# Half steps of the recurrence levels, 16-token blocks first, and two heads' matmuls in turn, in a hybrid decoder step

## The reference

```
s = einsum('btngd,btknd->btngk', q, k_sel) * 64**-0.5 ; p = softmax(s)      # attention over the chosen keys
o = einsum('btngk,btknd->btngd', p, v_sel)

b = cumsum(logf)                                                            # recurrence, one chunk
decay[t,s] = exp(b[t] - b[s])  for s <= t
scores[t,s] = sum_k q[t,k] k[s,k] decay[t,s,k]
o = scores @ v + (q * exp(b)) @ S0
S = exp(b_last) * S0 + (k * exp(b_last - b)).T @ v
```

## Time and profile before

| | us |
|---|---|
| median of 3 runs | 2303.99 |
| profiled execution | 2306.62 |
| its span, first to last instruction | 2304.8 |
| PE busy (92% of the span) | 2114.4 |
| DVE busy (52%) | 1201.4 |
| ACT busy (35%) | 809.1 |
| POOL busy (33%) | 759.9 |

### The profile page before, as it was taken

The page is one execution under the profiler, slowest core; times in us unless marked ns, Lnnn a source line. Parts: engine busy times, 40 slices in busy tenths (PEclk is TensorE's granted clock), DMA queues, the critical chain, the costliest instruction groups (busy, mean ns, idle before and its releaser), DMA issues. The chain is left out here.

```text
span 2304.8 us, 40432 instructions
## 1 busy us (share of the span) xinstructions
PE 2114.4 (92%) x15670; PEld 1981.7 (86%) x15670; DVE 1201.4 (52%) x2179; ACT 809.1 (35%) x1265; POOL 759.9 (33%) x414
## 2 busy tenths in 40 slices
PE   3999899977898999999999898998888899999998
PEld 2987799856688999999999778996667899999998
DVE  3385577776346543045347566876654564412533
ACT  3233222366333333222333332234543243422224
POOL 1642238200024343444355222651000343434433
PEclk9999999888789999999999999997877899999999
DMA  4322136101133322332241212441032323223222
GB/s 124 103 60 70 47 89 184 57 27 58 55 94 96 90 83 69 96 92 81 78 143 58 74 47 73 136 125 41 1 94 80 92 78 92 81 75 101 84 64 83
DMA packets 308923, 188.64 MB, mean 82 GB/s; under 512 B 15680, under 2 KB 295328, under 8 KB 307776
## 3 DMA queue, kind: packets, MB, share of 16 engines
q1 hardware_dynamic: 299168, 160.03, 24.5%
q0 software_dynamic: 4224, 16.78, 2.1%
q10 hardware_dynamic: 5408, 10.16, 1.3%
HBM read 167.47 MB, written 18.10 MB: 81 GB/s over the span
## 5 line engine op out<-in xcount | busy, mean ns | idle before, releaser
L635 POOL TENSOR_TENSOR w_lo<-raw,w_hi 128x1024 fp32r<-128x1024 f32 (+3 forms) x290 | 629.1, 2170 | 1422.5 <-ACT w_hi L1340 1422.2
L777 PE MATMUL acc<-normed,w_hi 128*128 128x268 f32 x5696 | 965.4, 292 | 22.1 <-POOL w_lo L635 20.7
L777 PEld LDWEIGHTS acc<-normed,w_hi 128*128 128x128 f32 x5696 | 809.2, 191 | 52.7 <-issue 28.0
L1340 ACT ACTIVATE w_hi<-raw 128x1024 fp32r<-128x1024 f32 (+1 forms) x290 | 293.1, 1011 | 978.0 <-PE acc L777 978.0
L777 PE MATMUL acc<-normed,w_lo 128*128 128x268 f32 x2848 | 589.0, 288 | 0.0
L777 PEld LDWEIGHTS acc<-normed,w_lo 128*128 128x128 f32 x2848 | 449.9, 191 | 0.0
L777 PE MATMUL acc<-hidden,w_hi 128*128 128x268 f32 x1408 | 237.4, 291 | 15.5 <-DVE hidden L2389 15.5
L777 PEld LDWEIGHTS acc<-hidden,w_hi 128*128 128x128 f32 x1408 | 202.4, 193 | 16.4 <-issue 16.4
L777 PE MATMUL acc<-hidden,w_lo 128*128 128x268 f32 x704 | 146.5, 290 | 0.0
L2389 DVE TENSOR_TENSOR hidden<-act_f,hidden 128x536 f32 x44 | 93.1, 2116 | 50.7 <-ACT hidden L1661 50.7
L2382 DVE TENSOR_TENSOR silu<-silu,rnorm 128x536 f32<-128x536 f32 x44 | 83.3, 1893 | 59.2 <-ACT silu L1658 59.2
(11 more groups left out here) (321 smaller groups left out, 2987.9 us busy)
## 6 DMA issues: line engine op xcount, KB each, us to landing
raw<-in_w_in_dram SPq DMA_DIRECT2D x90, 512.0 KB
raw<-in_w_gu_dram SPq DMA_DIRECT2D x88, 512.0 KB
raw<-in_w_down_dram SPq DMA_DIRECT2D x32, 384.0 KB
raw<-in_w_down_dram SPq DMA_DIRECT2D x32, 320.0 KB
gate_scratch<-gate_out ACTq DMA_DIRECT2D x32, 268.0 KB
normed<-gate_scratch SPq DMA_DIRECT2D x4, 2144.0 KB, 8.2
raw<-in_w_o_dram SPq DMA_DIRECT2D x16, 512.0 KB
raw<-in_w_pa_dram SPq DMA_DIRECT2D x16, 256.0 KB
```

The costliest lines, as they stand in the source:

```text
L635: pool.tensor_tensor(w_lo[s][:, 0:kt, :], raw[slot][:, 0:kt, :], w_hi[s][:, 0:kt, :].bitcast(f32), ALU.subtract).then_inc(lo_done, 1)
L777: mm = pe.matmul(acc[o][:, half, 0:HT], w[s][:, k, :], mov[:, part, k0 + k, half * HT:(half + 1) * HT], start=start and n == 0, stop=stop ...
L1340: act.activation(w_hi[slot % 2][:, 0:kt, :], raw[slot][:, 0:kt, :], ACT.Copy).then_inc(hi_done, 1)
```

## The change

There are four parts.

1. `level_diff`, `level_product` and `level_exp` take a `half` argument. The two halves are separate steps of the tables, and the exponent of a half no longer waits for the difference of the other. `decayed_keys` and `decayed_queries` are each split into two instructions of two heads.
2. The blocks run in another order (`BLK`): the four 16-token blocks first, then for each n2 the tiles 0 to 3.
3. The scores of the next block are issued behind `PE_AHEAD` instead of ahead of it. Both heads' scores, and both heads' value products, are issued in turn, key range by key range. Both heads' buffers are waited for first, and the waits for the tail and sample tiles in the scores are gone.
4. The tables have new places for all the level steps; tail copies are steps of their own.

```diff
+    BLK = [(n2, 4) for n2 in range(4)] + [(n2, j) for n2 in range(4) for j in range(4)]
-    PE_AHEAD = {1: [("diagonal", 0)], 2: [("diagonal", 1), ("level_tail", 7)], 4: [("level", 0, 0)], 5: [("level", 1, 0)],
...
+    PE_AHEAD = {1: [("diagonal", 0)], 2: [("diagonal", 1)], 4: [("level", 0, 0)], 6: [("level", 1, 0)],
...
-                 5: [("scores", 0, 1)], 6: [("scores", 1, 1), ("product", 2)], 7: [("scores", 2, 0), ("diff", 4)],
...
+                 4: [("tail", 7), ("diff", 1, 1)], 5: [("scores", 0, 1), ("diff", 2, 1)], 6: [("diff", 3, 0)],
...
-                def qk(h, j):
+                def qk(block):
+
+                    n2, j = BLK[block]
                     r0, n = TILES[j]
-                    s, step = h % 2, (h // 2) * 5 + j
-                    ps = acc[s][:, :, :].rearrange("p a b -> p (a b)")
-                    pe.wait_ge(qk_drained[s], L * 20 + step + 1)
+                    for s in range(2):
+                        pe.wait_ge(qk_drained[s], L * BLOCKS + block + 1)
                     hold(pe)
-                    if j == 4:
-                        wait(pe, "tail_drained", L, 5, 1 if step < 14 else 5)
-                        if step == 19:
-                            wait(pe, "sample_drained", L, 4, 2)
-                    kv, p0 = h // 2, 64 * (h % 2)
-                    key = A[p0:p0 + 64, 4 + kv // 2, :] if 64 * (kv % 2) == p0 else k_dup[p0:p0 + 64, kv // 2, :]
                     for c in range(0, WIDTH[j], 512):
                         w = min(512, WIDTH[j] - c)
-                        mm = pe.matmul(ps[0:n, c:c + w], A[p0:p0 + 64, h // 2, r0:r0 + n], key[:, c:c + w],
-                                       start=True, stop=True)
-                    mm.then_inc(qk_filled[s], 1)
+                        for s in range(2):
+                            p0 = 64 * s
+                            key = A[p0:p0 + 64, 4 + n2 // 2, :] if 64 * (n2 % 2) == p0 else k_dup[p0:p0 + 64, n2 // 2, :]
+                            mm = pe.matmul(acc[s][0:n, c // 512, 0:w], A[p0:p0 + 64, n2, r0:r0 + n], key[:, c:c + w],
+                                           start=True, stop=True)
+                            if c + w == WIDTH[j]:
+                                mm.then_inc(qk_filled[s], 1)
...
                     for s in range(2):
                         pe.wait_ge(turn_drained[s], L * BLOCKS + block + 1)
-                        for c in range(j + 1):
-                            w = min(P, WIDTH[j] - c * P)
+                    hold(pe)
+                    for c in range(j + 1):
+                        w = min(P, WIDTH[j] - c * P)
+                        for s in range(2):
                             mm = pe.matmul(ps[64 * s:64 * s + 64, 0:n], tok[0:w, c, 256 + n2 * 64:320 + n2 * 64],
                                            pT[0:w, s, c, 0:n], start=c == 0, stop=c == j)
...
                 for block in range(BLOCKS):
+                    rec_steps(PE_AHEAD.get(block, ()))
                     if block < BLOCKS - 1:
-                        nn, nj = (block + 1) // 5, (block + 1) % 5
-                        qk(2 * nn, nj)
-                        qk(2 * nn + 1, nj)
-                    rec_steps(PE_AHEAD.get(block, ()))
+                        qk(block + 1)
                     turn(block, 0)
...
-                def level_exp(lev):
-
-                    w = 512 if HALVES[lev] >= 16 else TP
-                    wait(act, "lev_diff", L, 14, 2 * lev + 2)
-                    act.activation(X[lev % 3][:, :, 0:w], X[lev % 3][:, :, 0:w], ACT.Exp).then_inc(S["lev_exp"], 1)
+                def level_exp(lev, half):
+
+                    hs, w = HALVES[lev], (512 if HALVES[lev] >= 16 else TP)
+                    wait(act, "lev_diff", L, 14, 2 * lev + half + 1)
+                    at = X[lev % 3][:, :, 0:w].rearrange("p h (b c) -> p h b c", c=2 * hs)
+                    at = at[:, :, :, 0:hs] if half else at[:, :, :, hs:]
+                    act.activation(at, at, ACT.Exp).then_inc(S["lev_exp"], 1)
...
-                def level_diff(lev):
+                def level_diff(lev, half):
...
-                    TT(xv[:, :, :, hs:], bv[:, :, :, hs:], mid, ALU.subtract).then_inc(S["lev_diff"], 1)
-                    TT(xv[:, :, :, 0:hs], mid, bv[:, :, :, 0:hs], ALU.subtract).then_inc(S["lev_diff"], 1)
-
-                def level_product(lev):
+                    if half == 0:
+                        TT(xv[:, :, :, hs:], bv[:, :, :, hs:], mid, ALU.subtract).then_inc(S["lev_diff"], 1)
+                    else:
+                        TT(xv[:, :, :, 0:hs], mid, bv[:, :, :, 0:hs], ALU.subtract).then_inc(S["lev_diff"], 1)
+
+                def level_product(lev, half):
```

More of the change, by code:

```diff
@@ L575, in _ @@
                     if h == 1:
-                        wait(sync, "q_decayed", L, 1, 1)
+                        wait(sync, "q_decayed", L, 2, 2)
                         hold(sync)
@@ L1071, in pv @@
                 def pv(block):
-                    n2, j = block // 5, block % 5
+                    n2, j = BLK[block]
                     n, ps = TILES[j][1], pv_tile()
@@ L1169, in chunk @@
                     ps = rec_begin(("decayed", c))
-                    wait(pe, "k_decayed", L, 1, 1)
+                    wait(pe, "k_decayed", L, 2, 2)
                     for h in range(4):
@@ L1508, in att_drain @@
                 def att_drain(block):
[L1510 removed]
+                    n2, j = BLK[block]
+                    r0, n = TILES[j]
                     wait(act, "pv_filled", L, BLOCKS, block + 1)
@@ L1576, in _ @@
                 for block in range(BLOCKS):
-                    j = block % 5
+                    j = BLK[block][1]
                     n, w = TILES[j][1], WIDTH[j]
@@ new lines, in level_product, with decayed_keys @@
+                def level_product(lev, half):
+                    xv, bv, qv, kv, hs, w = level_views(lev)
+                    wait(vec, "lev_exp", L, 14, 2 * lev + half + 1)
+                    if half == 0:
+                        TT(xv[:, :, :, hs:], xv[:, :, :, hs:], qv[:, :, :, hs:], ALU.mult).then_inc(S["lev_ready"], 1)
+                    else:
+                        TT(xv[:, :, :, 0:hs], xv[:, :, :, 0:hs], kv[:, :, :, 0:hs], ALU.mult).then_inc(S["lev_ready"], 1)
+                def decayed_keys(hp):
+                    at = slice(2 * hp, 2 * hp + 2)
+                    if hp == 0:
+                        wait(vec, "k_exp", L, 20, 20)
+                    TT(X1[:, at, :], X1[:, at, :], K[:, at, 0:TP], ALU.mult).then_inc(S["k_decayed"], 1)
@@ L2241, in make_v_blk, with decayed_queries @@
+                def decayed_queries(hp):
+                    at = slice(2 * hp, 2 * hp + 2)
+                    if hp == 0:
+                        wait(vec, "lev_ready", L, 14, 14)
+                        wait(vec, "decay_last", L, 1, 1)
+                    TT(B[:, at, 0:TP], X2[:, at, :], B[:, at, 0:TP], ALU.mult).then_inc(S["q_decayed"], 1)
                 def make_v_blk(h):
@@ L2272, in _ @@
                 rec_step = {"scan": scan, "diagonal": diagonal, "diff": level_diff, "product": level_product,
-                            "scores": level_scores, "tail": tail_scores, "v_blk": make_v_blk, "state": state_step, "sample_state": sample_state}
-                rec_once = {"keys": make_keys, "decayed_keys": decayed_keys, "decayed_queries": decayed_queries}
+                            "scores": level_scores, "tail": tail_scores,
+                            "decayed_keys": decayed_keys, "decayed_queries": decayed_queries, "v_blk": make_v_blk, "state": state_step, "sample_state": sample_state}
+                rec_once = {"keys": make_keys}
                 def rec_steps(steps):
```

68 lines of the change are left out of this document (29 added, 39 removed).

## The result

The changed kernel takes 2290.87 us in the median of 5 runs (2290.26 to 2297.76); the kernel before takes 2304.04 in the runs beside it. The ratio is 0.9944, with a 95% interval of 0.9922 to 0.9967. So it is faster by 13 us, and half of the forecast gain (26 us, to 2278) came. The time lies just above the forecast's own range (2266 to 2290) and inside the wider one that takes in the rivals (2260 to 2299); the nearest time that was named is rival (2)'s, 2294.

The account below looks back on a forecast made before the run. Waits in in-order queues bound the first part, TensorE the last. Layer 0 gains 10.3 + 2.6 = 12.9 us, layer 1 12.5 + 2.6 = 15.1, together 28.0: 2306.6 to 2278.6; forecast 2278, range 2266 to 2290.

Parts of the forecast that it names:

- rival (2): VectorE's queue is the bound: half the first part's gain, little of the last's, 6 us a layer, 2294; chance 0.12.
- First part, blocks 4 to 14: Blocks 4 to 13 hold the first part's gain: a level takes about 9 us instead of 11.
- 6.04 us tail wait: VectorE's wait for the last level-3 tail matmul, forecast to go once tails move with their first group.
- the sign named: VectorE's score copies (L2202) would wait for TensorE below 10 us in the first part, against 15.7 before.
- rival (3): Slower: TensorE gaps, most ahead of second level groups, and 16-token blocks in a row cost the clock; 2320, chance 0.08.
- First part, blocks 0 to 4: Four 16-token blocks at about 6.3 us each gain nothing; block 4's transposes at 32.3 us, 31.7 before.
- its test: The forecast is wrong if block 10 isn't at least 8 us earlier.
- Last part: Blocks 14 to 19: value products, transposes, scores and scaling sum to -2.6 us a layer.
- Half exponents: On ScalarE a half takes about 1.13 us, 2 us more a layer; the gain is in the order.
- Value products in turn: Two heads alternating overlap on TensorE: 16 records about 1.0 us, 12 about 0.8, 20 about 1.0.
- Scores behind the level groups: Levels 1 to 6 go to TensorE ahead of the next block's score matmuls; no gain taken for the scores.
- Outside the stage: The rest issues the same instructions in the same order, so the stage's gain comes out one for one.

Follow-up runs that it names:

- Experiment 3: Changed kernel plus TensorE matmuls of no use for the result, ahead of and behind the first scores and ahead of transposes of blocks 0 and 3; 2290.8 us.
- experiment 1: Changed kernel with the old order of the blocks, tail copies of levels 7, 3 and 6 moved by a step; 2278.3 us, ratio 0.9892.
- experiment 7: Changed kernel with one whole exponent per level at the place of its second half, products waiting for it; 2290.2 us, ratio 0.9928.
- Experiment 6: Changed kernel with the value products issued head by head again; 2297.1 us, ratio 0.996.
- Experiment 8: Changed kernel with the next block's scores issued ahead of the recurrence steps again; 2305.1 us, ratio 0.999.
- experiment 5: Changed kernel with the old block order plus useless matmuls ahead of the transposes of blocks 14, 15, 16, 18 and 19; 2269.8 us, ratio 0.985.

## Why the prediction was half right

- *First part, blocks 4 to 14.* Laid out at 63.7 us plus a share of the 2.5 us for slips; measured 65.3 (77.1 before). The 6.04 us tail wait is gone, the waits for level groups ahead of score copies fell from 15.7 to 10.3 us (the sign named was below 10), and one half difference stands in the chain. This step was right. TensorE's waits ahead of level groups are 3.9 us in all, none over 1.2, so neither rival (2) nor the gaps that rival (3) feared ahead of second groups made the shortfall.
- *First part, blocks 0 to 4: the step that failed.* The prediction put it: "The first four blocks gain nothing: the 16-token ones have the widest rows (528) and so the dearest chain, about 6.3 us each." Its layout had block 4 at 32.3 us, against 31.7 before; it came at 37.3, and layer 0's block 10 came 6.4 us earlier than before instead of the at least 8 that the prediction set as its test. The durations used were full-rate ones. With four 16-token blocks in a row at the start PE runs most of the opening at 1.2 GHz (mean clock 0.59, against 0.79 before): two groups of 16 records and 8 records of transposes take 3.78, 3.78 and 1.97 us. Experiment 3 gives 4.1 of the 5 us back with work that nobody needs, 3.0 with its cost ahead of the stage; experiment 1 gives 6.3. Why the clock stays low there isn't shown. PE does not stand idle for longer than before: 6.6 of 37.3 us, against 6.9 of 31.7, with 233 records instead of 160; no run separates the kind and size of these blocks' matmuls from their spacing. The prediction's remark that blocks 0 to 3 hold mostly transposes and small products said too much: transposes and value products are about 13 of the 30.7 busy us. With the old order the stage takes 170.0 and 171.9 us, and the median is 2278.3, the number of the forecast. That is in part luck: block 14 is where the forecast for the new order had it (99.1 and 101.3, against 98.5 and 100.0), but the last part is 1.8 us a layer shorter than forecast, and what lies outside the stages 1.8 us longer than before.
- *Rival (3)* named the place and the clock ("puts the 16-token blocks, with the least PE work, in a row"; PE's busy time there turned out larger than before, not smaller) and gave it 8 in 100, as something that would turn the result over. It happened in part: an own cost of about 5 us a layer at block 4, not a reversal. It belonged into the sum. Over both layers the stages fall 7.5 us short of the forecast's 28.0.
- *Last part.* Forecast -2.6 us a layer, measured -2.3 and -2.0. Right in size, but the terms aren't confirmed: the largest was -2.1 us for the value products, by order and by turn together, and issuing them head by head again costs only 0.6 and 0.5 us there; the old order has it 2 us shorter still, so having no 16-token block there brings nothing. That the sum came out is in part luck.
- *Half exponents.* Their duration (1.13 us by slope, 1.08 measured) was right; of the gain that the prediction gave to them together with the order, experiment 7 shows none that is theirs.
- *Value products in turn.* Taken as 1.0, 0.8 and 1.0 us, measured 0.86, 0.88 and 1.09. Experiment 6 gives 4.5 us a layer for them in the stages (3.1 by the medians), nearly all in the first part.
- *Scores behind the level groups.* The prediction moved them in its layout without pricing the move. Experiment 8 gives it 3.6 and 8.2 us a layer.
- *Outside the stage: counted at nothing, and it cost 4.8 us in the profiled pair.* The stages gave 8.6 and 11.9 us, 20.5 together, the profiled executions only 15.7 (2306.62 to 2290.87). Three stretches with the same instructions, before and after:

```profile
0.00:462.38 462.38, 402.69 (x2876) 371.08 (x2876) 283.66 (x686) 144.32 (x198) 176.48 (x111) 0.97 0.32 92
646.53:1581.85 935.32, 896.68 (x6807) 863.69 (x6808) 491.63 (x835) 296.40 (x375) 379.66 (x205) 0.97 0.31 89
1769.37:2304.80 535.43, 510.52 (x4012) 504.72 (x4012) 221.81 (x186) 171.78 (x206) 203.80 (x98) 0.97 0.30 87
```

```profile
0.00:463.70 463.70, 403.02 (x2875) 371.23 (x2876) 283.66 (x686) 144.35 (x198) 176.50 (x111) 0.97 0.32 91
639.27:1576.44 937.17, 898.55 (x6807) 865.46 (x6808) 491.34 (x835) 296.44 (x375) 380.03 (x205) 0.96 0.31 89
1752.06:2289.10 537.04, 512.91 (x4012) 506.73 (x4012) 221.87 (x186) 171.80 (x206) 203.82 (x98) 0.96 0.30 87
```

They are 1.3, 1.9 and 1.6 us longer, with the same instructions (one record more or less) and at a clock lower by up to 0.01. The spread between executions is enough for this: in the other kernels of this study the stage of layer 0, with nothing changed ahead of it, begins anywhere from 462.9 to 470.3 us, and the three stretches add up to 1933.0 us in experiment 5's profiled execution and to 1942.6 in experiment 6's, against 1933.1 before and 1937.9 after. Experiment 5's stages are 17 and 20 us shorter than before the change, so a shorter stage doesn't by itself make the rest longer. With the 7.5 us of the stages the 4.8 make up the 12.3 us by which the profiled execution lies above the forecast's 2278.6.

Open is how experiment 1's gain divides between clock and chain. Experiments 1 and 3 show that the order of the blocks costs it, and that the clock is more than half of the delay at block 4; why filling the gaps there brings nothing in the median isn't settled.

## What to carry to other kernels

A reorder that changes which TensorE work stands together must be priced at the clock that this stretch will have; durations read at the full clock are too short where it will be at half. In this kernel the 16-token blocks were cheaper spread among the others than collected at the start. Where PE waits 2 to 3 us again and again, cheap matmuls into a free tile can be worth more than reordering (19 us here, in the last part; in the opening they brought nothing in the median), and matmuls that could share the array should alternate in the queue.

## What the runs showed of the hardware

- Two heads' value products in distinct column halves of the array: 16 records take 1.58 us head by head and 1.09 in turn; 20 records of 16 columns 1.60 and 0.86. The Trainium skill, "TensorE: Matmul & The Clock Gate", Part 3, says that matmuls placed in distinct column groups of the array run concurrently. The traces agree in part: in turn 31% and 46% of these times are saved, and the 8 records of a 256-wide block take 0.66 us either way.
- 80 matmuls more in two layers (160 records) made a kernel 19 us faster; the mean clock of the last part rose from 0.69 to 0.81 in layer 0.
- The same instructions ahead of the stage took 6.6 us longer in one execution than in another (470.3 us in experiment 6's kernel, 463.7 in the changed one), at a mean clock of 0.95 against 0.97.
